# A mixture-of-experts kernel: expert results added to the tokens in PSUM by one-hot products, gate and up in two passes, down in fp32

## The reference

```python
g_p, g_idx = lax.top_k(jax.nn.softmax(g_logits, axis=-1), 1)          # one of 4 groups
e_top, e_idx = lax.top_k(e_logits, TOP_K_IN_GROUP)                     # two of its 8 experts
gate = g_p * jax.nn.softmax(e_top, axis=-1)                            # a weight per assignment
def expert_block(args):
    xb, e = args
    return (jax.nn.silu(xb @ w_gate[e]) * (xb @ w_up[e])) @ w_down[e]  # 1024 -> 256 -> 1024
y_rows = y_rows * row_w[:, None].astype(y_rows.dtype)
out = jnp.zeros((T + 1, D), y_rows.dtype).at[row_token].add(y_rows)[:T]
```

## Time and profile before

| | us |
|---|---|
| median of 3 runs (range) | 1017.51 (1015.9 to 1023.0) |
| the profiled execution, its own time | 1019.81 |
| its span, first to last instruction | 1018.0 |
| busy: TensorE products / weight loads | 902.0 (89%) / 724.0 (71%) |
| busy: DVE / ACT / POOL | 489.2 (48%) / 424.9 (42%) / 143.9 (14%) |
| mean granted TensorE clock | 0.913 |
| HBM read / written | 183.07 MB / 11.01 MB |

### The profile page before, as it was taken

The page is one execution under the profiler, slowest core; times in us unless marked ns, Lnnn a source line. Parts: engine busy times, 40 slices in busy tenths (PEclk is TensorE's granted clock), DMA queues, the critical chain, the costliest instruction groups (busy, mean ns, idle before and its releaser), DMA issues.

```text
span 1018.0 us, 13414 instructions
## 1 busy us (share of the span) xinstructions
PE 902.0 (89%) x4944; PEld 724.0 (71%) x4944; DVE 489.2 (48%) x599; ACT 424.9 (42%) x533; POOL 143.9 (14%) x128
## 2 busy tenths in 40 slices
PE   5976996959999999499999998789999999999966
PEld 4864775449999998368788873557777777777742
DVE  1004434135666666310201032438998887787742
ACT  2112214135454544212110011138788778778740
POOL 0000000012424243200200000002212211212100
PEclk9997555979999999689699999699999999999998
DMA  9872000214545454213134344018999999999923
GB/s 373 293 195 93 0 1 0 98 69 169 203 170 202 168 203 169 79 62 145 42 131 158 131 159 165 1 65 337 352 358 359 348 360 361 350 358 358 352 86 121
DMA packets 29200, 194.54 MB, mean 191 GB/s; under 512 B 3736, under 2 KB 3992, under 8 KB 7536
## 3 DMA queue, kind: packets, MB, share of 16 engines
q1 hardware_dynamic: 25488, 182.56, 48.0%
q0 software_dynamic: 3680, 11.54, 4.0%
HBM read 183.07 MB, written 11.01 MB: 191 GB/s over the span
## 4 chain that ended last, share of the span: by engine, by line
PE 67%; ACT 9%; DVE 9%; issue 7%; DMA 5%; POOL 1%; ACTq 1%; DVEq 0%; POOLq 0%
PE psum L608 30%; PE psum L450 10%; PE psum L473 6%; ACT expert_w_high L373 5%; DMA line_scratch<-arena 4%; PE psum L458 3%; DVE expert_w_low L378 3%; PE psum L757 3%; PE psum L438 2%; ACT xw_high L921 2%; ACT junk L902 1%; PE psum L793 1%; ACTq L1074 1%; PE psum L550 1%; PE psum L580 1%
## 5 line engine op out<-in xcount | busy, mean ns | idle before, releaser
L378 DVE TENSOR_TENSOR expert_w_low<-ring,expert_w_high 128x2048 fp32r<-128x2048 f32 x64 | 158.0, 2471 | 49.3 <-ACT expert_w_high L373 49.2
L373 ACT ACTIVATE expert_w_high<-ring 128x2048 fp32r<-128x2048 f32 x64 | 121.7, 1904 | 31.2 <-DVE HT L1522 31.2
L450 PE MATMUL psum<-HT,ring 128*128 128x256 f32 x592 | 131.5, 384 | 0.0
L450 PEld LDWEIGHTS psum<-HT,ring 128*128 128x128 f32 x592 | 113.5, 193 | 17.2 <-issue 1.6
L378 DVE TENSOR_TENSOR ffn_w_low<-ring,ffn_w_high 128x2048 fp32r<-128x2048 f32 x33 | 80.2, 2432 | 68.1 <-ACT ffn_w_high L373 68.1
L921 ACT ACTIVATE arena<-psum 64x1024 f32<-64x1024 f32 (+5 forms) x50 | 41.1, 835 | 144.3 <-PE psum L608 43.4
L608 PE MATMUL psum<-ht_high,ffn_w_high 128*128 128x256 f32 x352 | 100.1, 284 | 1.1 <-DVE ffn_w_low L378 1.1
L608 PE MATMUL psum<-ht_low,ffn_w_high 128*128 128x256 f32 x352 | 99.8, 283 | 0.0
L608 PE MATMUL psum<-ht_high,ffn_w_low 128*128 128x256 f32 x352 | 99.7, 283 | 0.0
L373 ACT ACTIVATE ffn_w_high<-ring 128x2048 fp32r<-128x2048 f32 x33 | 63.1, 1915 | 86.9 <-PE psum L608 86.7
L608 PE MATMUL psum<-expert_w_high,xw_high 128*64 128x256 f32 x264 | 75.1, 284 | 4.9 <-issue 3.1
(11 more groups left out here) (281 smaller groups left out, 1559.9 us busy)
## 6 DMA issues: line engine op xcount, KB each, us to landing
ring<-units_in SPq DMA_DIRECT2D x165, 1024.0 KB, 5.1
results_scratch<-arena POOLq DMA_DIRECT2D x32, 256.0 KB, 4.0
const<-const_in SPq DMA_DIRECT2D x1, 2112.0 KB, 13.9
arena<-results_scratch SPq DMA_DIRECT2D x4, 512.0 KB, 5.2
rows<-rows_in SPq DMA_DIRECT2D x1, 1688.0 KB, 23.9
line_scratch<-arena POOLq DMA_DIRECT2D x1, 1536.0 KB, 36.5
small<-small_in SPq DMA_DIRECT2D x1, 1236.0 KB, 16.5
X<-x_in SPq DMA_DIRECT2D x1, 1024.0 KB, 4.8
```

The source lines that it names most:

```text
L373: nc.scalar.activation(parts_slot(n)[0], w, ACT.Copy).then_inc(hi_ready, 1)
L378: nc.vector.tensor_tensor(l, ring[:, n % RING, :], h.bitcast(fp32), SUB).then_inc(lo_ready, 1)
L450: last = mm(psum[:, bank, half * S:half * S + S], w[:, k * stride + half * P:k * stride + half * P + P], HT[:, k, :], start=k == 0, stop=k ...
```

## The change

- The results no longer go through DRAM. A table made by four small fp32 products (`RH` by `RW`) gives, for each expert's 64 ranks, the token and the weight; each row stands twice, on partitions 0 to 63 and 64 to 127. DVE makes from it a one-hot matrix of the expert's tokens (`tokens_of`, 128x256); ACT takes the down results times the weight as fp32r (`high_results`), DVE their remainder on partitions 64 to 127 (`low_results`); and `scatter` adds both to all 256 tokens in PSUM banks 4 to 7, four fp32r products of 512 columns for each expert, one turn later. X is added once, at the end.
- Gate and up in two passes: the high and low window stand side by side as one stationary matrix of 128 columns, multiplied with the high and the low part of the weights, 16 products a unit instead of 24. The low window's results come out on partitions 64 to 127; ACT copies these down (`low_rows`) and DVE adds (`sum_halves`) ahead of silu and activations. There is one bank for gate and up, bank 0, and `up_summed` frees it.
- Down in fp32: the unit straight from the ring, four products of 128x128 by 128x512; no split of down. ACT writes the transposed activations twice side by side (`turned`). Down has one pair of banks, 2 and 3.
- Split slots: gate alternates between two, up has one.
- WP, CT and the listing of extra passes in the loop go (the listing runs only if there are any). The constants grow by 226 columns.

Some loop counts and names of semaphores are left out below.

```diff
-        XWH, XWL = (sb(f"xw_{part}", [P, 2, KD, CH], f32r) for part in ("high", "low"))
+        XW = sb("xw", [P, 2, KD, 2 * CH], f32r)
...
-            AEH, AEL = parts_tensor("ae", (2, 2, CH))
+            YH = space.enter_context(nc.sbuf_tensor("weighted", [P, 2, D], f32r))
+            W = space.enter_context(nc.sbuf_tensor("token_onehot", [P, 2, S], f32r))
             EWH, EWL = parts_tensor("expert_w", (2, UNIT))
...
+        def gate_of(e):
+            return U_EXP if e == 0 else U_EXP - 1 + 3 * e
+        def down_of(e):
+            return UNITS - 1 if e == EXPERTS - 1 else U_EXP + 4 + 3 * e
         def parts_slot(n):
             if n < U_GLA:
                 return FWH[:, n % 2, :], FWL[:, n % 2, :]
-            k = (n - U_EXP) % 3
-            return (third_high[:, :], third_low[:, :]) if k == 2 else (EWH[:, k, :], EWL[:, k, :])
+            if n != U_EXP and (n - U_EXP) % 3 != 2:
+                return EWH[:, 1, :], EWL[:, 1, :]
+            e = (n - U_EXP + 1) // 3
+            return (EWH[:, 0, :], EWL[:, 0, :]) if e % 2 == 0 else (third_high[:, :], third_low[:, :])
...
+                e = (n - U_EXP) // 3
+                return gate_of(e - 1) + 2 if e >= 1 else None
+            e = (n - U_EXP + 1) // 3
+            return gate_of(e - 2) + 1 if e >= 2 else None
...
-            sp.wait_ge(results_in_dram, 1)
-            for s in range(SB):
-                sp.dma_start(YS[:, s, :], results_dram[s * P:(s + 1) * P]).then_inc(ys_loaded[s], 16)
...
-            pe.wait_ge(wp_ready, 1)
-            for s in range(SB):
-                for tt in range(TT):
-                    last = nc.tensor.transpose(psum[:, 6 + s // 2, (s % 2) * S + tt * P:(s % 2) * S + (tt + 1) * P],
-                                               WP[:, tt, s * P:(s + 1) * P], ident)
-            last.then_inc(ct_done, 1)
-            pe.wait_ge(ct_sb, 1)
...
-            def expert_up(par, g, x, w, ks=range(KD)):
+            def expert_up(g, x, w, ks=range(KD)):
                 for k in ks:
-                    last = by_parts(psum[0:CH, par, g * D_EXP:(g + 1) * D_EXP], [v[:, k, :] for v in x],
-                                    [v[:, k * D_EXP:(k + 1) * D_EXP] for v in w], k == 0, k == KD - 1)
+                    for part in w:
+                        last = mm(psum[:, 0, g * D_EXP:(g + 1) * D_EXP], x[:, k, :],
+                                  part[:, k * D_EXP:(k + 1) * D_EXP], start=k == 0 and part is w[0],
+                                  stop=k == KD - 1 and part is w[-1])
...
-            def expert_down(par, x, w):
+            def expert_down(w):
                 for n in range(2):
                     for f in range(2):
                         a = f * D + n * 512
-                        last = by_parts(psum[0:CH, (2, 6)[par] + n, :], [v[:, f, :] for v in x],
-                                        [v[:, a:a + 512] for v in w], f == 0, f == 1)
+                        last = mm(psum[:, 2 + n, :], AE[:, f, :], w[:, a:a + 512], start=f == 0, stop=f == 1)
                 return last
+            def scatter(par, tt, bank, first=False, final=False):
+                for n in range(2):
+                    last = mm(psum[:, bank + n, :], W[:, par, tt * P:(tt + 1) * P], YH[:, par, n * 512:(n + 1) * 512],
+                              start=first, stop=final)
+                return last
...
             def experts(e, i=0):
                 if e < EXPERTS - 1:
-                    par = (e + 1) % 2
-                    x = XWH[:, par], XWL[:, par]
                     pe.wait_ge(xw_lo, i * 2 + (e + 2))
-                    expert_up(par, 0, x, parts(U_EXP + 2 + 3 * e, i)).then_inc(unit_used, 1)
-                    w = parts(U_EXP + 3 + 3 * e, i)
+                    pe.wait_ge(up_summed, i * 2 + (e + 1))
+                    expert_up(0, XW[:, (e + 1) % 2], parts(gate_of(e + 1), i)).then_inc(unit_used, 1)
+                    w = parts(gate_of(e + 1) + 1, i)
                 pe.wait_ge(at_ready, i * 2 + (e + 1))
                 if e < EXPERTS - 1:
-                    expert_up(par, 1, x, w, range(1))
-                expert_turn(e % 2).then_inc(at_tr, 1)
+                    expert_up(1, XW[:, (e + 1) % 2], w, range(1))
+                expert_turn().then_inc(at_tr, 1)
                 if e < EXPERTS - 1:
-                    expert_up(par, 1, x, w, range(1, KD)).then_inc(unit_used, 1)
-                pe.wait_ge(ae_lo, i * 2 + (e + 1))
-                if e >= 2:
-                    pe.wait_ge(y_copied, i * 2 + (e - 1))
-                expert_down(e % 2, (AEH[:, e % 2], AEL[:, e % 2]),
-                            parts(U_EXP + 4 + 3 * e if e < EXPERTS - 1 else UNITS - 1, i)).then_inc(unit_used, 1)
+                    expert_up(1, XW[:, (e + 1) % 2], w, range(1, KD)).then_inc(unit_used, 1)
+                if e >= 1:
+                    pe.wait_ge(y_lo, i * 2 + e)
+                    for tt in range(TT):
+                        last = scatter((e - 1) % 2, tt, 4 + 2 * tt, first=e == 1)
+                    last.then_inc(scattered, 1)
+                w = unit(pe, down_of(e), i)
+                pe.wait_ge(ae_ready, i * 2 + (e + 1))
+                expert_down(w).then_inc(unit_used, 1)
             pe.wait_ge(xw_lo, 1)
             for g in range(2):
-                expert_up(0, g, (XWH[:, 0], XWL[:, 0]), parts(U_EXP + g)).then_inc(unit_used, 1)
+                expert_up(g, XW[:, 0], parts(U_EXP + g)).then_inc(unit_used, 1)
+            pe.wait_ge(table_in, 1)
+            table(2 * P).then_inc(table_done, 1)
...
+            pe.wait_ge(y_lo, EXPERTS)
+            for tt in range(TT):
+                scatter((EXPERTS - 1) % 2, tt, 4 + 2 * tt, final=True).then_inc(y_done, 1)
...
-            for tt in range(TT):
-                for s in range(SB):
-                    pe.wait_ge(ys_loaded[s], 16)
-                    for n in range(2):
-                        last = mm(psum[:, 2 * tt + n, :], CT[:, s, tt * P:(tt + 1) * P],
-                                  YS[:, s, n * 512:(n + 1) * 512], start=s == 0, stop=s == SB - 1)
-                last.then_inc(y_done, 1)
...
+            def low_rows(e, i=0):
+                act.wait_ge(unit_used, i * RING + (gate_of(e) + 2))
+                copy(TS[0:CH, :], psum[CH:P, 0, :]).then_inc(low_half, 1)
+            def silu(e, i=0):
+                act.wait_ge(up_summed, i * 2 + (e + 1))
+                nc.scalar.activation(SL[0:CH, :], UG[0:CH, 0:D_EXP], ACT.Silu).then_inc(silu_done, 1)
+            def turned(e, i=0):
+                act.wait_ge(at_tr, i * 2 + (e + 1))
+                copy(AE.rearrange("p f (d n) -> p f d n", d=2),
+                     psum[:, 1, 0:2 * CH].rearrange("p (f n) -> p f n", f=2).unsqueeze(2).to_broadcast([P, 2, 2, CH])
+                     ).then_inc(ae_ready, 1)
+            def high_results(par, weight):
+                return nc.scalar.activation(YH[:, par, :], psum[:, 2:4, :].rearrange("p a b -> p (a b)"), ACT.Copy,
+                                            scale=TW[:, ds(weight, 1)])
             def results(e, i=0):
-                act.wait_ge(unit_used, i * 6 + (U_EXP + 5 + 3 * e if e < EXPERTS - 1 else UNITS))
+                if e == 0:
+                    act.wait_ge(table_sb, 1)
+                act.wait_ge(unit_used, i * RING + (down_of(e) + 1))
                 if e >= 2:
-                    act.wait_ge(y_stored, i * 32 + 16 * (e - 1))
-                b = (2, 6)[e % 2]
-                copy(YO[0:CH, e % 2, :], psum[0:CH, b:b + 2, :].rearrange("p a b -> p (a b)")).then_inc(y_copied, 1)
+                    act.wait_ge(scattered, i * 2 + (e - 1))
+                high_results(e % 2, i * 2 + (EXPERTS + e)).then_inc(y_hi, 1)
             def experts(e, i=0):
-                if e < EXPERTS - 1:
-                    split_hi(act, U_EXP + 2 + 3 * e, i)
-                act.wait_ge(unit_used, i * 6 + (U_EXP + 2 if e == 0 else U_EXP + 1 + 3 * e))
-                silu(e % 2).then_inc(silu_done, 1)
-                if e < EXPERTS - 1:
-                    split_hi(act, U_EXP + 3 + 3 * e, i)
-                if e == EXPERTS - 1:
-                    split_hi(act, UNITS - 1)
                 if e >= 1:
                     results(e - 1, i)
                 if e < EXPERTS - 2:
                     window_hi(e + 2, i)
+                    split_hi(act, gate_of(e + 2), i)
+                turned(e, i)
                 if e < EXPERTS - 1:
-                    split_hi(act, U_EXP + 4 + 3 * e, i)
-                act.wait_ge(at_tr, i * 2 + (e + 1))
-                copy(AEH[:, e % 2], psum[:, 4 + e % 2, 0:2 * CH].rearrange("p (f n) -> p f n", f=2)).then_inc(ae_hi, 1)
+                    low_rows(e + 1, i)
+                if e < EXPERTS - 2:
+                    split_hi(act, gate_of(e + 2) + 1, i)
+                if e < EXPERTS - 1:
+                    silu(e + 1, i)
...
+            split_hi(act, gate_of(1))
+            low_rows(0)
+            split_hi(act, gate_of(1) + 1)
+            silu(0)
...
```

(68 more changed lines are left out.)

262 lines of the change are left out of this document (140 added, 122 removed).

## The result

| | kernel before | changed kernel |
|---|---|---|
| median | 1019.92 us (4 runs, 1015.9 to 1023.0) | 983.22 us (4 runs, 979.34 to 985.15) |
| ratio, 95% interval | | 0.9627 [0.9602, 0.9652] |
| profiled execution, its span | 1019.81, 1018.0 | 979.34, 977.4 |

The changed kernel is 36.7 us faster by the medians, where 41.3 were forecast. The forecast was 976 us for the median and 978.5 for the profiled execution; the median lies 7.2 above it. Of these 7.2, 4.6 are gain that did not come. The rest is the starting point: the forecast took off 2.3 us because the profiled execution (1019.81) lay that much above the median of three runs, 1017.51, and with a fourth run that median is 1019.92.

A forecast was written before the change was run, and what follows sets the result against it. The prediction took the down matrix's split, in series with its use, as the bound (9.55 us a turn). Gains of 1.2 at the start, 23.3 in the loop and 16.8 at the end made 41.3: 976 us, range 966 to 1000.

The forecast's parts named there:

- The bound before: Expert loop before the change: the down matrix's split on ACT and DVE, in series with its use, sets 9.55 us a turn.
- TensorE's turn, 8.69: Expert loop after the change: TensorE's gate, up, transposes, down and scatter sum to 8.69 us a turn and become the bound.
- the columns' least time (8.0): Lower bound of TensorE's turn in the loop, from column counts at 2.4 GHz: 8.0 us; trace rows were used instead.
- ACT 6.9 and DVE 7.7: Expert loop: summed work of ACT 6.9 us and DVE 7.7 us a turn, both under TensorE's 8.69.
- The slacks: Waits inside a loop turn: 2.0 us to spare ahead of gate, 1.0 ahead of up; low results ready before scatter.
- The loop of two turns: Longest dependency loop through TensorE, ACT and DVE: 16.3 us for two turns, 8.2 a turn.
- Rival B, the loads: Weight loads bind the loop: a turn of 8.84 us and 981 us, or 9.57 and 1002; chance 0.18.
- Rival C, the hand-offs: Ten links of the two-turn loop cost 0.2 to 0.3 us each: turn 9.0 to 9.5, 985 to 1000 us; chance 0.13.
- Rival D: Single gate/up bank serialises the loop behind a late DVE: turn 10.4, 1028 us, slower than before; chance 0.05.
- The start: Before the loop: removed transposes worth 0, first products at 678.50, down(0) ends at 693.8 instead of 695.0, gain 1.2 us.
- if the granted clock falls in the loop: Failure sign for the loop: TensorE's granted clock, taken as 1.00, drops there; no size given.
- The end: After the last down: no DRAM store and reload, first X addition at 964.5, span ends at 976.7, gain 16.8 us.

The follow-up runs named there:

- e5: Kernel before with only down changed, to four fp32 products straight from the ring without a split of down: 1025.67 us, ratio 1.0053.
- e4: Changed kernel plus one unused 128x1024 addition on DVE in each turn, behind the sum of the halves: 988.01 us.
- e8: Changed kernel without gate/up products of the weights' low halves and without DVE's low splits for the experts: 956.96 us.
- e7: Changed kernel without gate/up products of the weights' low halves, DVE's low splits kept: 958.99 us.
- e6: Kernel before with only gate and up in two passes, down still split, results still by DRAM: 1086.64 us, ratio 1.0658.
- e9: Kernel before with gate and up in two passes, silu and activations one split later as in the changed kernel: 1041.74 us, ratio 1.022.
- e1: Changed kernel plus one unused fp32 product on TensorE behind the gather: 979.41 us, ratio 0.9586.
- e2: Changed kernel plus four unused fp32 products behind the gather: 979.72 us, ratio 0.959.
- e3: Changed kernel plus four unused products behind the gather and three ahead of the first up product: 980.54 us, ratio 0.9604.
- e12: Changed kernel plus one unused product behind the gather, measured again beside the changed kernel: 979.74 us, ratio 0.9606.

## Why the prediction was right, and where it was off

**The bound before.** "The bound is the split of the down matrix, in series with its use": e5 takes that split away, and TensorE becomes full at once, at 9.71. Right. But that turn is 0.16 longer than the old one: the split's place was taken by what fp32 adds to TensorE.

**TensorE's turn, 8.69.** Measured 8.62, in all 22 turns from 753.02 to 942.66. By terms: down 3.43 for 3.50 (0.86 a product for 0.875); gate, up and transposes 4.26 for 4.20; scatter 0.93 for 0.99. Taking the rows rather than the columns' least time (8.0) was right.

**ACT 6.9 and DVE 7.7.** The groups sum to 6.95 and 7.30; DVE's two splits ran 2.29, not the mean of 2.47. The unknown ones were priced well: low rows 0.60 (0.65), the sum 0.68 (0.67), the high results 1.12 (1.02), which is 0.1 more.

**The slacks.** Ahead of `up`: 1.0 forecast, 1.0 by e4. Ahead of the scatter: 1.9 forecast. In the changed kernel the low results of a turn end at 759.22 and the scatter starts at 760.71, 1.5 later:

```profile
757.93 1.29 DVE L1678 SCALAR_TENSOR_TENSOR weighted<-psum,arena,weighted 64x1024 fp32r<-64x1024 f32 x1 [0.49 <-ACT weighted L1130]
```

It was over-estimated by 0.4, since the results' operations and the hand-offs ran longer, and it still covered. (e8's loop of 7.74 would leave 0.9, but with TensorE's terms as they are behind a wait, 3.69 and 1.21, not 3.43 and 0.93.) The loop of two turns was right: 8.2 a turn, by e7 too.

**Rival B, the loads.** 364 GB/s were enough, at a share of 0.96, and 400 were to be had (e7). The rule weighed in the prediction (the Trainium skill, "DMA: Bandwidth & Descriptors", "Where 436 GB/s comes from", some 358 GB/s from HBM) is contradicted here by both numbers, with one core streaming; the skill's "HBM Reference", section "Specifications (TRN2)", states that a core streaming alone measures well above its share, and the runs agree.

**Rival C, the hand-offs.** They cost 0.04 to 0.19 us each in e8, not 0.2 to 0.3, and stay off the path.

**Rival D.** Its mechanism is real where DVE is late: e6 and e9 are slower than before through the new sum's waits, and in part through the lower granted clock. In the changed kernel, with two splits instead of three, DVE is never late.

**The start, the step that failed.** The sum took 32 products "x 0.12" and said that the removed transposes "are worth 0". They cost nothing in time and did something else: with 1.04 us of them behind the gather, TensorE kept its speed; without them it idles 3.90 us, and the next 5.7 us of products run at 1.2 GHz, as do those behind the second hole of 2.81. The 15.3 us came out as 21.9: 2.6 on the first 32 products with their hand-off (the split starts 7.1 after the first product, not 4.5), 0.9 from there to the end of `activations`, 2.2 on the second `up` and 1.0 on down(0). The one filler of e1 takes 5.4 of the 6.6 back. The prediction named "if the granted clock falls in the loop" as what would make it fail, and didn't look at the hole ahead of it, of which 3.06 us stood in the earlier trace rows. (The Trainium skill, "TensorE: Matmul & The Clock Gate", "What's actually happening", says that the slow level is the default and activity releases the fast one. The runs agree: 0.21 against 0.12 us between the same products.)

**The end.** 15.5 us from the last down to the end of the span, 15.3 forecast; the first addition comes 3.3 after the last down (965.17 less 961.89), 3.1 forecast.

## What to carry to other kernels

When two resources are within a few per cent of each other, an edit that relieves the binding one can lose time by what it adds to the other: sum a turn for every engine after each part of a change, not only after the whole. Cheap products that stand in a gap can be what keeps TensorE's clock up, so before removing them from ahead of a dependent chain, write down how long TensorE would then be idle; one unused product of 1 us at that place gave back 5.4 us at the start here, and 3.2 of the median. A moved wait costs by what is queued behind it: the same arithmetic in another issue order was 45 us apart, a part of it through TensorE's lower granted clock (0.88 against 0.97).

## What the hardware showed that was not expected

- A hole of a few us changed TensorE's level for longer than it lasted. At the start TensorE kept the upper level behind 3.05 us of idle time (e1; 3.06 before) and had lost it behind 3.90; both profiles of the changed kernel show the same 6.61 us for the 32 products. At the last turn, behind the same hole of 2.26 or 2.27 us, three profiles kept the level (the changed kernel's two and e4) and six lost it (e1, e2, e3, e7, e8, e12); the length of a hole alone does not tell.
- DVE's `activations` on 64x256 took 1.31 us instead of 0.41 where it ran beside POOL's window:

```profile
685.74 1.31 DVE L1696 TENSOR_TENSOR arena<-arena 64x256 f32<-64x256 f32 x1
```

```profile
685.68 1.09 POOL L1261 TENSOR_TENSOR xw<-arena,xw 128x512 fp32r<-128x512 f32 x1 [10.28 <-ACT xw L958]
```

  Both read two operands in SBUF, and DVE's ends 0.28 us after POOL's (686.77). It fits what the Trainium skill says in "SBUF — State Buffer", "Who interferes with whom", of such a pair: one waits for the other's whole instruction. The runs bear it out: in e8, where DVE's split is left out, `activations` is done at 687.83 and POOL's window starts at 688.01, and it takes 0.42; in e7, with the overlap back, 1.31. It is also the only one of the changed kernel's 32 that overlaps a POOL operation, and the others take 0.41 or 0.42.
- An fp32 product of 512 columns costs 0.86 us with a stationary side 128 wide (3.43 for four) and 0.90 with one 64 wide (3.58 for four, e5): the narrower one is no cheaper.
